# A four-layer mixer network on one core: the conditioning products, each quarter of TensorE given its own columns

## The chip, the cores and the metric

The kernel runs on one NeuronCore of a Trainium2 chip. The metric is the device time of one execution in microseconds (us). The kernel is written out by hand for five instruction queues: TensorE (PE, with its weight loads shown as PEld), VectorE (DVE), ScalarE (ACT), GpSimd (POOL) and SyncE (SP), which issues most of the DMAs. The queues meet at semaphores only; each runs its own list in order.

## The reference

A sequence of 256 latent tokens and 256 context tokens of width 1024 goes through four conditioned layers and then two more sublayers on the latent tokens (a mixer of three branches and a feed-forward net). The four conditioned layers differ in their mixer (window attention, latent attention, mLSTM, window attention) but share one frame:

```
def rmsnorm(x, g):
    xf = x.astype(jnp.float32)
    y = xf * lax.rsqrt(jnp.mean(xf * xf, axis=-1, keepdims=True) + EPS)
    return (y * g.astype(jnp.float32)).astype(x.dtype)
```

Each layer has a matrix `w_ada` of 1024 x 3072 and a bias `b_ada`. Two vectors (one for the latent tokens from `c`, one for the context tokens from `c_ctx`) go through silu and are multiplied with `w_ada`. The 3072 results are, for each of the two, a shift, a scale and a gate of 1024 each. Before the mixer the normalised rows become `norm(x) * (1 + scale) + shift`; after it, its normalised output is multiplied by the gate and added to `x`. The whole is in float32.

The change concerns only how the product with `w_ada` is laid out and turned.

## The kernel before

**Weights.** All weights pass through a ring of six slots (`NR`), in blocks of 512 KB, [128, 1024] float32. SyncE's `w_load` loads block j when block j - 6 has been used. For ordinary blocks ScalarE rounds a high part (`w_h`, `w_round`) and VectorE makes the rest (`w_l`, `w_rest`); conditioning blocks are used raw. `Weights.next` hands out a block and lets the splits run up to `ahead` blocks ahead, so a split that comes early waits in ScalarE's queue for its load. The first 15 blocks of layer 0's conditioning lie in places of their own (`aside`).

**The product.** Only two of the rows of the stationary operand carry anything: `cT` is [128, 8, 32], with two used columns, one for each condition. A matmul of 32 stationary columns fills a quarter of TensorE's columns and writes 32 partitions. `ada_mm` (L2235) puts four such products into the four quarters, each with other rows (another k of 128) of the same 256 columns. A block holds four k and 256 columns. Four blocks (two halves of columns, two sets of rows) fill a group's bank of 512 columns, with four partial sums on partitions 0, 32, 64, 96 (and 1, 33, 65, 97 for the context). float32 products go through TensorE in two passes, so a block shows as eight weight loads.

**After it.** Groups 0 to 3 of a layer are shift and scale: ScalarE copies the bank to `stage` (`ada_row`), and `ada_turn` (L2242) makes four products with `stage` as the stationary operand and the two-column selector `sel` as the moving one, which adds the four partial sums and puts the columns on partitions. VectorE adds the bias and the gain in `ada_add` (L2909). Groups 4 and 5 are the gate: ScalarE copies them to `gt_rows`, a DMA puts the bias on row 2, `gate_split` makes a high part `l_gth` (ScalarE) and a rest `gt_rest` (VectorE), both [128, 1024], and `gate_spread` (L2249) multiplies a broadcast selector with both to put the sum on all partitions, 512 columns at a time, four times a layer; VectorE multiplies each by the gain into `l_G`.

**Order.** The generator `ada` (L533) yields after each block and is woven by `weave` into the units of an attention: `weave(att, ada, num, den)` lets `num` steps of `ada` run per `den` units and drains what is left at the end. It runs in the second attention call of layer 0 (gate of 0, shift and scale of 1), in layer 1's attention (gate of 1, rest of 2), among the mLSTM chunks of layer 2 (`paced` by two; gate of 2, rest of 3) and in the second attention call of layer 3 (gate only, 10 steps to 16 units). Turns come `lag` steps after their group, gate steps 0 to 4 come 10, 12, 14, 16 and 18 steps after the gate's second group. All take one of the two banks PAIR = (0, 1), one of which a group in progress holds. Layer 0's own shift and scale are computed at the start (`layer_first`), group by group, between the first rows and the first products of layer 0.

## Time and profile before

| | us |
|---|---|
| median of three runs | 1579.5 (1578.32 to 1583.96) |
| the profiled execution | 1581.7 |
| its span, first to last instruction | 1579.9 |
| TensorE busy | 1483.3 (94%) |
| VectorE busy | 1000.6 (63%) |
| ScalarE busy | 766.0 (48%) |
| mean granted TensorE clock | 0.984 of full |

Busy time counts an instruction from its start to its end; on TensorE the ends are modelled and neighbours overlap, so what an operation costs there is read from one start of a weight load to the next. "Granted clock" is the share of the full TensorE clock of 2.4 GHz. A row's bracket says how long the engine stood before it and who released it; "issue" is no wait on another engine. A row's line number can be that of a helper (L2207 all products, L2210 all transposes, L2515 ScalarE copies, L2872 VectorE operations on two tensors), so operations are told apart by tile names.

### The profile page before, as it was taken

How to read it: one execution, taken by the hardware profiler on the slowest of the kernel's cores; microseconds unless marked ns; L12 is line 12 of the kernel's file. 1: busy time of each engine (PE TensorE's matmuls, PEld its weight loads, DVE VectorE, ACT ScalarE, POOL GpSimd, SP SyncE). 2: the span in 40 equal slices, each digit the busy share in tenths (PEclk: the TensorE clock that was granted, in tenths of full speed). 3: DMA queues.
4: the chain of work that ended last, by engine and by line, in shares of the span. 5: the costliest groups of instructions: out<-in, count | busy, mean ns of one | idle time of the engine just before them, and what ended most of it. 6: DMA issues, size and time to landing. Idle time of an engine off the chain costs nothing.

```text
span 1579.9 us, 24093 instructions
## 1 busy us (share of the span) xinstructions
PE 1483.3 (94%) x9344; PEld 1205.7 (76%) x9344; DVE 1000.6 (63%) x2304; ACT 766.0 (48%) x1640; POOL 67.5 (4%) x76
## 2 busy tenths in 40 slices
PE   6999998999999999999998999888899999989999
PEld 4787756787778777888766777666687789789987
DVE  3647677464667458635576667666786557777753
ACT  4436576353556344332224545565666437455542
POOL 0000000010000000020000100001100120000000
PEclk9999999999999999999989999999999999999999
DMA  9131172222452232221371134423435552445554
GB/s 358 55 107 54 50 244 95 76 92 80 138 184 94 70 111 93 91 83 54 123 264 53 54 130 126 144 84 123 152 133 160 182 182 94 147 156 191 188 187 134
DMA packets 59842, 202.84 MB, mean 128 GB/s; under 512 B 7682, under 2 KB 10956, under 8 KB 59600
## 3 DMA queue, kind: packets, MB, share of 16 engines
q1 hardware_dynamic: 53568, 192.84, 35.6%
q10 hardware_dynamic: 5984, 7.40, 2.0%
q8 instruction: 75, 1.23, 0.3%
q0 software_dynamic: 176, 1.06, 0.2%
q14 instruction: 39, 0.32, 0.1%
HBM read 199.42 MB, written 1.84 MB: 127 GB/s over the span
## 4 chain that ended last, share of the span: by engine, by line
PE 72%; DVE 15%; ACT 5%; DMA 3%; issue 3%; POOL 1%; ACTq 0%; SPq 0%; POOLq 0%; DVEq 0%
PE ps L2207 66%; PE ps L2210 5%; DVE w_l L2872 3%; DMA w_raw<-in_l_out 1%; DVE st L2968 1%; ACT w_h L2515 1%; DVE x L2880 1%; DVE l_h_lat L2880 1%; DMA w_l_ada<-in_l_ada 1%; DVE m_P L3452 1%; ACT l_P L2518 1%; DVE l_xn L2876 1%; DMA w_raw<-in_l_z 1%; DVE l_P L2876 1%; POOL mstat L3546 0%
## 5 line engine op out<-in xcount | busy, mean ns | idle before, releaser
L2872 DVE TENSOR_TENSOR w_l<-w_raw,w_h 128x1024 fp32r<-128x1024 f32 (+3 forms) x263 | 314.8, 1206 | 76.6 <-ACT w_h L2515 76.1
L2515 ACT ACTIVATE w_h<-w_raw 128x1024 fp32r<-128x1024 f32 (+3 forms) x263 | 271.3, 1042 | 112.9 <-DMA w_raw<-in_l_out 26.3
L2207 PE MATMUL ps<-w_h,l_hTh 128*128 128x512 f32 (+1 forms) x384 | 157.2, 410 | 0.3 <-DVE w_l L2872 0.2
L2207 PE MATMUL ps<-w_h,l_hTl 128*128 128x512 f32 (+1 forms) x384 | 152.8, 398 | 0.0
L2207 PE MATMUL ps<-w_l,l_hTh 128*128 128x512 f32 (+1 forms) x384 | 152.7, 398 | 0.0
L2518 ACT ACTIVATE l_P<-ps,st 128x512 f32<-128x512 f32 (+1 forms) x128 | 77.5, 607 | 82.3 <-DVE st L2880 55.0
L2207 PE MATMUL ps<-f_hTh,w_h 128*128 128x256 f32 x352 | 99.0, 281 | 0.0
L2207 PE MATMUL ps<-f_hTl,w_h 128*128 128x256 f32 x352 | 98.9, 281 | 0.0
L2207 PE MATMUL ps<-f_hTh,w_l 128*128 128x256 f32 x352 | 98.9, 281 | 0.0
L2968 DVE TENSOR_REDUCE st<-ps 128x1 f32<-128x512 f32 (+2 forms) x112 | 72.8, 650 | 40.4 <-PE ps L2207 39.7
L2207 PE MATMUL ps<-l_hTh,w_h 128*128 128x512 f32 (+1 forms) x264 | 97.5, 369 | 0.5 <-issue 0.5
L2207 PE MATMUL ps<-l_hTl,w_h 128*128 128x512 f32 (+1 forms) x264 | 96.9, 367 | 0.0
L2207 PE MATMUL ps<-l_hTh,w_l 128*128 128x512 f32 (+1 forms) x264 | 96.9, 367 | 0.0
L2207 PEld LDWEIGHTS ps<-w_h,l_hTl 128*128 128x128 f32 x384 | 73.3, 191 | 16.7
L2207 PEld LDWEIGHTS ps<-w_h,l_hTh 128*128 128x128 f32 x384 | 73.5, 191 | 15.2 <-issue 1.2
L2207 PEld LDWEIGHTS ps<-w_l,l_hTh 128*128 128x128 f32 x384 | 73.4, 191 | 14.5
L2207 PE MATMUL ps<-l_PT,l_V 128*64 128x128 f32 (+1 forms) x712 | 69.9, 282 | 3.1 <-DVE l_ogf L2880 3.1
L2207 PEld LDWEIGHTS ps<-l_PT,l_V 128*64 128x64 f32 (+1 forms) x712 | 55.6, 151 | 21.4 <-issue 13.4
L2210 PE MATMUL ps<-cst,l_P 128*128 128x128 f32 x416 | 67.1, 281 | 4.5 <-ACT l_PT L2515 1.7
L2207 PEld LDWEIGHTS ps<-f_hTh,w_h 128*128 128x128 f32 x352 | 67.1, 190 | 0.2 <-issue 0.2
L2207 PEld LDWEIGHTS ps<-f_hTl,w_h 128*128 128x128 f32 x352 | 67.0, 190 | 0.0
L2207 PEld LDWEIGHTS ps<-f_hTh,w_l 128*128 128x128 f32 x352 | 66.9, 190 | 0.0
(444 smaller groups left out, 3484.4 us busy)
## 6 DMA issues: line engine op xcount, KB each, us to landing
w_raw<-in_l_ada SPq DMA_DIRECT2D x81, 512.0 KB, 4.3
w_raw<-in_l_z SPq DMA_DIRECT2D x32, 512.0 KB, 3.6
w_raw<-in_l_out SPq DMA_DIRECT2D x32, 512.0 KB, 3.7
w_raw<-in_m_merge SPq DMA_DIRECT2D x24, 512.0 KB, 3.3
w_raw<-in_f_gate SPq DMA_DIRECT2D x22, 512.0 KB, 3.3
w_raw<-in_f_up SPq DMA_DIRECT2D x22, 512.0 KB, 3.3
w_raw<-in_f_down SPq DMA_DIRECT2D x22, 512.0 KB, 4.3
w_raw<-in_l_q SPq DMA_DIRECT2D x16, 512.0 KB, 3.7
```

What stands on the lines that cost most here:

```text
L2207: return p.e.matmul(out, lhsT, rhs, start=start, stop=stop)
L2210: return p.e.transpose(out, a, ident)
L2515: return p.e.activation(out, a, func, scale=scale)
L2518: return p.e.activation(out, a, func, bias=bias, scale=scale, accum_out=accum)
L2872: return p.e.tensor_tensor(out, a, b, op)
L2876: return p.e.tensor_scalar(out, a, s1, None, op0)
L2880: return p.e.scalar_tensor_tensor(out, a, s, b, op0, op1)
L2968: p.e.reduce_max(soft.stat(u, 0, nh), ps if nh == 1 else ps.rearrange("p (h k) -> p h k", h=nh), AX.X).then_inc(*p.mark(*soft.key("peak", u)))
L3452: v = p.e.tensor_tensor_reduce(dst, src, bias[i], 1.0, -3.0e38, ALU.add, ALU.max, mx[:, i:i + 1])
```

## The change

A block of shift and scale holds k outermost: one k of 1024 columns (512 of shift, 512 of scale) in layers 1 to 3, two k of 512 columns (256 and 256) in layer 0. The four quarters of TensorE work on the same k and on different columns: 256 each in layers 1 to 3, 128 each in layer 0. The eight k are summed in the bank, so that a group of eight blocks (four in layer 0) uses 256 (128) columns of it, and a layer has two groups (layer 0 four). Partition 32 j + v has the results of quarter j for condition v. The turn is a transpose of each 128 columns (two in a group, one in layer 0), from which VectorE takes the columns that matter through a strided view. The gate is one group of eight blocks, [128, 256]; its bias goes to partitions 2, 34, 66, 98; its high part and rest are 256 wide, and a spread makes four products of 256 columns with a selector for quarter and condition. The generator yields after every second block, `lag` is 2 of these steps, gate steps come one after another, and the weaves have 14 steps in each of the three attentions; layer 2's is no longer paced. In layer 0's opening the order is kept. Left out below: the size of `selr`, the file's other changed call of `aside`.

```diff
+ADA = (256, 512, 512, 512)
...
-    ada = [_r(o + 256 * b, o + 256 * b + 256) for b in range(4) for o in (0, 1024)] + _split(_r(2048, 3072), 256)
+    both = lambda a, b: np.concatenate([_r(a, b), _r(1024 + a, 1024 + b)])
-        add(f"l{i}_ada", f"l{i}_w_ada", ada, 4, D)
+        add(f"l{i}_ada", f"l{i}_w_ada", [both(a, a + ADA[i]) for a in range(0, 1024, ADA[i])], 1024 // (2 * ADA[i]), D)
+        add(f"l{i}_adg", f"l{i}_w_ada", [_r(2048, 3072)], 1, D)
...
-    sel = np.zeros((128, 2), np.float32)
-    sel[[0, 32, 64, 96], 0] = 1
-    sel[[1, 33, 65, 97], 1] = 1
+    sel = np.zeros((128, 8), np.float32)
+    for j in range(4):
+        for lc in range(2):
+            sel[[32 * j + lc, 32 * j + 2], 2 * j + lc] = 1
-    c["selb"] = sel + np.where(np.arange(128) == 2, 1, 0)[:, None].astype(np.float32)
...
-        self.gt, self.gtl = self.at("gt_rows", [128, D], F32, at), self.at("gt_rest", [128, D], F32R, at)
+        self.gt, self.gtl = self.at("gt_rows", [128, 256], F32, at), self.at("gt_rest", [128, 256], F32R, at)
...
-    def ada(p, pool, groups, gate=None, steps=(), lag=2, ahead=AHEAD, blocks=(), late=None):
+    def ada(p, pool, groups, gate=None, lag=2, ahead=AHEAD, blocks=(), late=None):
...
-        for i, b in groups:
+        for i, g in groups:
-            for half in range(2):
-                for r in range(2):
-                    x = (2 * b + half) * 2 + r
-                    c = blocks.pop(0) if blocks else p.W.next(f"l{i}_ada", x, 4, 256, raw=True, ahead=ahead)
-                    key = ("ada", "mm", i, x)
-                    p.ada_mm(key, c, bank, half, r)
-                    c.free = key
+            w = 256 if g == "gate" else ADA[i] // 2
+            name, ks = f"l{i}_ada" if g != "gate" else f"l{i}_adg", 256 // w
+            nb = 8 // ks
+            for r in range(nb):
+                x = r if g == "gate" else g * nb + r
+                c = blocks.pop(0) if blocks else p.W.next(name, x, ks, 4 * w, raw=True, ahead=ahead)
+                key = ("ada", "mm", i, g, r)
+                p.ada_mm(key, c, bank, r, ks, w)
+                c.free = key
+                if r < nb - 1 and (late is not None or r % 2):
-                    if late is None or half + r < 2:
-                        yield
-            if b < 4:
+                    yield
+            if g != "gate":
-                v = ("ada", "row", i, b)
-                p.ada_row(v, bank, s, key, p.stage_tok[s])
-                then = lambda i=i, b=b, s=s, v=v: p.ada_mod(i, b, s, v, pool)
+                v = ("ada", "row", i, g)
+                p.ada_row(v, bank, s, w, key, p.stage_tok[s])
+                then = lambda i=i, g=g, s=s, v=v, w=w: p.ada_mod(i, g, s, w, v, pool)
-                v = ("ada", "gate_row", i, b)
-                p.ada_gate_row(v, bank, b, key)
+                v = ("ada", "gate_row", i)
+                p.ada_gate_row(v, bank, key)
-            if b == 5:
+            if g == "gate":
-                wait += [[10 + 2 * x, lambda x=x: gate.step(x, pool)] for x in steps]
-            if late is not None:
-                yield
+                wait += [[5 + x, lambda x=x: gate.step(x, pool)] for x in range(5)]
+            tick()
+            yield
-    def ada_mod(p, i, b, s, v, pool):
+    def ada_mod(p, i, g, s, w, v, pool):
-        p.stage_tok[s] = ("ada", "col", i, b)
-        p.ada_turn(p.stage_tok[s], mb, s, v)
-        t, u, w = ("ada", "shift", i, b), ("ada", "scale0", i, b), ("ada", "scale", i, b)
-        p.ada_add(t, u, w, i, b, mb, p.stage_tok[s])
+        p.stage_tok[s] = ("ada", "col", i, g)
+        p.ada_turn(p.stage_tok[s], mb, s, w, v)
+        t, u, x = ("ada", "shift", i, g), ("ada", "scale0", i, g), ("ada", "scale", i, g)
+        p.ada_add(t, u, x, i, g, w, mb, p.stage_tok[s])
-        p.mod_ready[i, b] = [t, w]
+        n = w // 128
+        for kp in range(n * g, n * g + n):
+            p.mod_ready[i, kp] = [t, x]
     def staged(p, n_units, lead, ring, soft, peak, cols, late, lag=1, early=True):
...
-        gpost, gth = at("gpost", [128, D], F32, gpost), at("gth", [128, D], F32R, gth)
+        gpost, gth = at("gpost", [128, D], F32, gpost), at("gth", [128, 256], F32R, gth)
...
-        groups = [(i, 4), (i, 5)] + ([(i + 1, b) for b in range(4)] if i < 3 else [])
+        groups = [(i, "gate")] + ([(i + 1, 0), (i + 1, 1)] if i < 3 else [])
-        weave(att, p.ada(PAIR, groups, Gate(p, i, *gate, f), range(5), lag=3), 4 * len(groups) + 2, steps)
+        weave(att, p.ada(PAIR, groups, Gate(p, i, *gate, f)), 14, steps)
...
-        weave(m.attention(f), p.ada(PAIR, [(1, 4), (1, 5)] + [(2, b) for b in range(4)], gate, range(5), lag=3), 28, 32)
+        weave(m.attention(f), p.ada(PAIR, [(1, "gate"), (2, 0), (2, 1)], gate), 14, 32)
...
-        mod = paced(p.ada(PAIR, [(3, 0), (3, 1), (2, 4), (2, 5), (3, 2), (3, 3)], gate, range(5), lag=3, ahead=2), 2)
+        mod = p.ada(PAIR, [(3, 0), (2, "gate"), (3, 1)], gate, ahead=2)
...
-    def ada_mm(p, key, c, bank, half, r):
+    def ada_mm(p, key, c, bank, r, ks, w):
-        p.wait_ge(c.ready, ("begin", "cT"), p.B.freed[bank] if half + r == 0 else None)
-        for j in range(4):
-            m = p.mm(n.ps[32 * j:32 * j + 32, bank, half * 256:half * 256 + 256], n.cT[:, 4 * r + j, :], c.raw[:, j], r == 0, r == 1)
+        p.wait_ge(c.ready, ("begin", "cT"), p.B.freed[bank] if r == 0 else None)
+        for s in range(ks):
+            k = ks * r + s
+            for j in range(4):
+                m = p.mm(n.ps[32 * j:32 * j + 32, bank, 0:w], n.cT[:, k, :], c.raw[:, s, w * j:w * j + w], k == 0, k == 7)
-    def ada_turn(p, key, mb, s, v):
+    def ada_turn(p, key, mb, s, w, v):
-        for j in range(4):
-            m = p.mm(out[:, 2 * j:2 * j + 2], n.stage[s][:, j * 128:j * 128 + 128], n.c["sel"], True, True)
+        for j in range(w // 128):
+            m = p.tr(out[:, 128 * j:128 * j + 128], n.stage[s][:, j * 128:j * 128 + 128], n.c["ident"])
     def gate_spread(p, gate, bank, lc, b, tok, g):
-        n, i, c = p.n, gate.i, slice(b * 512, b * 512 + 512)
-        sel = n.selr[:, lc:lc + 1].to_broadcast([128, 128])
+        n, i = p.n, gate.i
-        p.mm(n.bank(bank), sel, gate.gth[:, c], True, False)
-        p.wait_ge(("gate", "l", i))
-        p.mm(n.bank(bank), sel, n.gtl[:, c], False, True).then_inc(*p.mark(*tok))
+        for y in range(2):
+            j, out = 2 * b + y, n.bank(bank)[:, 256 * y:256 * y + 256]
+            sel = n.selr[:, 2 * j + lc:2 * j + lc + 1].to_broadcast([128, 128])
+            p.mm(out, sel, gate.gth[:], True, False)
+            p.wait_ge(("gate", "l", i))
+            m = p.mm(out, sel, n.gtl[:], False, True)
+        m.then_inc(*p.mark(*tok))
     def rows_turn(p, rows, ts, kp, b):
...
-    def ada_row(p, key, bank, s, tok, stage_tok):
+    def ada_row(p, key, bank, s, w, tok, stage_tok):
-        p.copy(p.n.stage[s][:], p.n.bank(bank)).then_inc(*p.mark(*key))
-    def ada_gate_row(p, key, bank, b, tok):
+        p.copy(p.n.stage[s][:, 0:w], p.n.bank(bank, w)).then_inc(*p.mark(*key))
+    def ada_gate_row(p, key, bank, tok):
-        p.copy(p.n.gt[:, b * 512 - 2048:b * 512 - 1536], p.n.bank(bank)).then_inc(*p.mark(*key))
+        p.copy(p.n.gt[:], p.n.bank(bank, 256)).then_inc(*p.mark(*key))
-        row = p.n.dram[f"l{i}_b_ada"].unsqueeze(0)[:, 2048:3072]
+        rows = p.n.dram[f"l{i}_b_ada"][2048:3072].rearrange("(j c) -> j c", j=4)
-        p.e.dma_start(p.n.gt[2:3, :], row).then_inc(*p.landed("d_gate_bias", i))
+        p.e.dma_start(p.n.gt[2:99:32, :], rows).then_inc(*p.landed("d_gate_bias", i))
...
-        p.copy(n.selr[:], n.c["selb"]).then_inc(*p.mark("begin", "const"))
+        p.copy(n.selr[:], n.c["sel"]).then_inc(*p.mark("begin", "const"))
...
-    def ada_add(p, t, u, w, i, b, mb, tok):
-        n, mod, out, k = p.n, p.n.mod[i % 2], p.n.bank(mb), slice(2 * b, 2 * b + 2)
-        bc = lambda name: n.v[name][:, k].unsqueeze(2).to_broadcast([128, 2, 2])
-        pv = out[:, 0:8].rearrange("p (a k v) -> p a k v", a=2, v=2)
+    def ada_add(p, t, u, x, i, g, w, mb, tok):
+        n, c = p.n, w // 128
+        k = slice(2 * c * g, 2 * c * g + 2 * c)
+        mod, out = n.mod[i % 2][:, :, k], n.bank(mb)[:, 0:w].rearrange("p (c a q y) -> p a c q y", c=c, a=2, q=2)
+        to = mod.rearrange("p a (q c) v -> p a c q v", q=2)
+        bc = lambda name: n.v[name][:, k].unsqueeze(2).to_broadcast([128, 2 * c, 2])
+        of = lambda name: bc(name).rearrange("p (q c) v -> p c q v", q=2)
-        p.tt(mod[:, 0, k], pv[:, 0], bc(f"l{i}_b_sh"), ALU.add).then_inc(*p.mark(*t))
-        p.tt(mod[:, 1, k], pv[:, 1], bc(f"l{i}_b_sc"), ALU.add).then_inc(*p.mark(*u))
+        p.tt(to[:, 0], out[:, 0, :, :, 0:2], of(f"l{i}_b_sh"), ALU.add).then_inc(*p.mark(*t))
+        p.tt(to[:, 1], out[:, 1, :, :, 0:2], of(f"l{i}_b_sc"), ALU.add).then_inc(*p.mark(*u))
-        p.stt(mod[:, 1, k], mod[:, 1, k], 1.0, bc(f"l{i}_g_pre"), ALU.add, ALU.mult).then_inc(*p.mark(*w))
+        p.stt(mod[:, 1], mod[:, 1], 1.0, bc(f"l{i}_g_pre"), ALU.add, ALU.mult).then_inc(*p.mark(*x))
     def gate_split(p, gate, gt_tok):
```

## Rows read from the trace of the kernel before

**Rows 1.** The page, chain of work that ended last, shares by engine.
```profile
PE 72%; DVE 15%; ACT 5%; DMA 3%; issue 3%; POOL 1%; ACTq 0%; SPq 0%; POOLq 0%; DVEq 0%
```

**Rows 2.** Stages: length, busy of PE, PEld, DVE, ACT, POOL, clock, DMA share, GB/s.
```profile
20.00:52.00 32.00, 29.85 (x217) 21.59 (x216) 16.84 (x36) 15.20 (x25) 0.00 (x0) 1.00 0.69 269
202.00:236.00 34.00, 33.46 (x335) 20.11 (x334) 26.83 (x96) 25.67 (x82) 0.00 (x0) 1.00 0.78 268
...
423.00:500.00 77.00, 76.92 (x630) 58.91 (x629) 53.17 (x190) 45.18 (x125) 0.00 (x0) 1.00 0.53 177
...
817.00:833.00 16.00, 13.22 (x94) 9.49 (x86) 11.50 (x25) 9.22 (x15) 0.00 (x0) 0.79 0.58 205
...
1047.00:1054.00 7.00, 4.24 (x23) 2.79 (x20) 4.24 (x10) 4.41 (x6) 0.00 (x0) 0.87 0.01 2
```

**Rows 3.** Timeline of TensorE's weight loads, layer 0's second attention call.
```profile
207.61 0.42 PEld L2210 LDWEIGHTS ps<-cst,l_P 128*128 128x128 f32 x4 [0.41 <-DVE l_P L2876]
...
208.78 0.16 PEld L2207 LDWEIGHTS ps<-w_raw,cT 128*32 128x32 f32 x8 [0.24 <-issue]
209.35 0.42 PEld L2210 LDWEIGHTS ps<-cst,l_P 128*128 128x128 f32 x4 [0.41 <-DVE l_P L2876]
209.74 0.19 PEld L2207 LDWEIGHTS ps<-l_kTh,l_qT 128*128 128x128 f32 x1
...
217.84 0.19 PEld L2207 LDWEIGHTS ps<-l_kTh,l_qT 128*128 128x128 f32 x1
217.96 0.19 PEld L2207 LDWEIGHTS ps<-l_kTl,l_qT 128*128 128x128 f32 x1
218.29 0.16 PEld L2207 LDWEIGHTS ps<-w_raw,cT 128*32 128x32 f32 x8
...
222.61 0.59 PEld L2207 LDWEIGHTS ps<-w_raw,cT 128*32 128x32 f32 x16
223.61 0.85 PEld L2207 LDWEIGHTS ps<-l_PT,l_V 128*64 128x64 f32 x16 [0.41 <-DVE l_ogf L2880]
```

**Rows 4.** The same timeline, layer 1's attention.
```profile
462.77 0.97 PEld L2207 LDWEIGHTS ps<-cst,stage 128*128 128x128 f32 x8 [0.41 <-issue]
463.65 0.97 PEld L2207 LDWEIGHTS ps<-l_PT,l_V 128*128 128x128 f32 x8
...
477.56 0.18 PEld L2207 LDWEIGHTS ps<-l_gth,selr 128*128 128x128 f32 x1 [0.41 <-issue]
...
477.90 0.64 PEld L2207 LDWEIGHTS ps<-l_PT,l_V 128*128 128x128 f32 x4
```

**Rows 5.** A ScalarE copy of 128x128 out of a bank: duration in ns, min/median/max.
```profile
L2515 ACT ACTIVATE m_bv<-ps x2: 268/272/277, 1107.6 to 1108.3; 128x128 f32<-128x128 f32 x2
```

**Rows 6.** The chain in order of time, layer 0's opening.
```profile
34.55 0.60 ACT stage L2515
...
35.20 1.05 PE ps L2207 x8
```

**Rows 7.** The chain in order of time, end of layer 3's second attention call.
```profile
1048.44 0.95 ACT l_gth L2515
...
1049.42 1.24 DVE gt_rest L2872
...
1051.24 0.70 DVE l_G L2872
```

**Rows 8.** Weight loads, end of layer 0's second attention call.
```profile
256.98 0.18 PEld L2207 LDWEIGHTS ps<-l_gth,selr 128*128 128x128 f32 x1 [1.56 <-DVE l_G L2872]
...
260.67 0.97 PEld L2207 LDWEIGHTS ps<-cst,stage 128*128 128x128 f32 x8 [1.59 <-ACT stage L2515]
```

**Rows 9.** Weight loads, first product of layer 3's output projection.
```profile
1053.33 0.33 PEld L2207 LDWEIGHTS ps<-w_h,l_qT 128*128 128x128 f32 x1
```

**Rows 10.** Timeline of VectorE, layer 0's second attention call.
```profile
208.17 0.16 DVE L2880 SCALAR_TENSOR_TENSOR st<-st,l_sink 128x1 f32<-128x1 f32 x1
...
209.75 0.16 DVE L2880 SCALAR_TENSOR_TENSOR st<-st,l_sink 128x1 f32<-128x1 f32 x1
```

More of the change, by code:

```diff
@@ L278, in place @@
         self.identb = self.at("identb", [128, 128], BF16, self.here(256))
-        self.selr = self.new("selr", [128, 2], F32R)
+        self.selr = self.new("selr", [128, 8], F32R)
         self.phalf = self.new("phalf", [128, 8])
@@ L668, in layer_first @@
         places = [base + 1024 * k for k in (52, 56, 60, 64, 68, 72, 76, 80, 84, 88, 92, 96, 115, 119, 123)]
-        blocks, late = [p.W.aside("l0_ada", x, 4, 256, at) for x, at in enumerate(places)], []
+        blocks, late = [p.W.aside("l0_ada", x, 2, 512, at) for x, at in enumerate(places)], []
         p.begin_loads(blocks)
```

## The prediction

> **What bounds the kernel now.** I read the chain of work that ended last first: 72% of the span is TensorE [rows 1], so what counts is time taken from TensorE where it is the last to arrive, and from ScalarE or VectorE only where they are. Then the table of stages [rows 2] for the five places in which the conditioning (the "ada" work) is done: the opening of layer 0 (20 to 52 us), the second attention call of layer 0 (202 to 262), the attention of layer 1 (423 to 500), the mLSTM chunks of layer 2 (to 833) and the second attention call of layer 3 (to 1054). In 423 to 500 TensorE is busy 76.92 of 77 us, in 202 to 236 33.46 of 34: there every TensorE nanosecond counts. After 236 the gate steps load VectorE too and I take the bound as mixed. In 1047 to 1054 TensorE works 4.24 of 7 us: something is waited for. Last, the weight-load timeline of TensorE, since start to start of loads is what an operation costs there (the durations of matmuls include their latency).
>
> **Part 1: two blocks per step.** The matmuls for layers 1 to 3 and for the gates stay the same in number and shape (four quarters, 32 stationary and 256 moving columns); only the meaning of a quarter changes. A lone block takes 0.57 us, 208.78 to the next load at 209.35; two in a row take 1.00 us, 222.61 to 223.61 [rows 3]. So the block proper is 0.43 and leaving the quarter layout costs 0.14. Entering costs too: two loads of the scores lie 0.12 apart (217.84, 217.96), but the ada block after them starts 0.33 later: 0.21. A pair therefore saves 0.14 + 0.21 = 0.35 us, where full-width work stands on both sides. Where the next work is the value product of layer 0 with its 64-column tiles, a change of layout is paid anyway, and I take 0.14. Before, a step has one block: layer 0 has 24 blocks in 23 runs (the pair at 222.61 is its one double step), layer 1 24 in 24, layer 3 8 in 8; after: 12, 12 and 4 runs. Layer 2 had its steps paced by two already and gains nothing here. Layer 1: 12 x 0.35 = 4.2. Layer 0: 11 fewer, about half of each kind, 11 x 0.25 = 2.8. Layer 3: 4 x 0.25 = 1.0. The weights come as before in 512 KB blocks, six slots ahead. The DMA share of 0.78 in 202 to 236 [rows 2] leaves room for a step of two blocks every 1.7 attention units, so I cost the transfers at nothing; without that cover each late pair would stand in TensorE's queue and hold the scores behind it.
>
> **Part 2: the turn.** Before, four groups per layer, each four fp32 products with two columns, eight loads: 462.77 to 463.65 = 0.88 us [rows 4]. After, layers 1 to 3 have two groups, each two transposes of 128x128. Four such transposes take 209.35 to 209.74 = 0.39 [rows 3], so two take 0.2. Per layer 4 x 0.88 - 2 x 0.2 = 3.1 us of TensorE in layers 0 (for layer 1's weights) and 1. In layer 2 the last turn runs where the granted clock was 0.79 of full [rows 2], so I take 3.6. ScalarE's copies ahead of it go from four of 128x512 to two of 128x256: between 0.27 (a 128x128 copy, [rows 5]) and 0.60 [rows 6]; I take 0.38.
>
> **Part 3: the gate.** Gate rows are 256 wide on 128 partitions instead of 1024 wide: one copy of about 0.38 instead of two of 0.60, the high part 0.95 becomes about 0.4 and the rest 1.24 becomes about 0.4 [rows 7] (estimates, by size between the same rows). The spread becomes four products of 256 columns instead of two of 512: before 477.56 to 477.90 = 0.34 us [rows 4], after 4 x 0.12 (spacing of 256-column products, [rows 3]) = 0.48. That is +0.14, four times a layer: +0.55. The products into G on VectorE (0.70, [rows 7]) stay. The bias comes in one DMA as before, four rows of 1 KB, four steps ahead of its use: nothing. In layer 1 the load of the post gains is still issued with gate step 0 and has one step of 2.3 units where it had two of 1.1: nothing either.
>
> **Part 4: order.** Gate steps now come one step apart instead of two and start after step 8 of about 14. Two consequences. In layers 0 and 1, spread 1 and the turn of the first group fall into the same step, while the running group holds the other of the two PAIR banks, so the turn waits until VectorE has multiplied the spread; behind it in TensorE's queue stand the next unit's transposes and scores, and VectorE's next maximum waits for those. Waits of that kind were up to 1.56 us [rows 8]; I take +1.0 in each of layers 0 and 1. In layer 3 the pace was 10 steps for 16 units, so gate split and spreads came after the attention, with nothing beside them: high part from 1048.44, rest from 1049.42 [rows 7], first product of the output projection at 1053.33, with a load of 0.33 instead of 0.19 [rows 9, 3], that is at the half clock. After, the gate steps fall on yields 9 to 14 of about 22 and are woven in. TensorE may start the output at about 1048.8: 4.5 us, and about 1.0 for the half clock at the start. Against that, VectorE gets 4 x 0.70 + 0.4 = 3.2 us inside an attention that is already bound by the three engines in turns. At the end of layer 0's call the last turn waited 1.59 us for its copy [rows 8]; it now falls inside the weave: -1.6.
>
> **Part 5: opening of layer 0.** Four groups as before; each block has eight products of 128 columns instead of four of 256. On the chain each group has a copy of 0.60 and a turn of 1.05 [rows 6]. After: copy 0.27, one transpose 0.1 plus the same latency, about 0.27. So 1.1 per group. The first group's gain I give to the wait for the next weights, with DMA at 0.69 of its time in this stretch [rows 2]; three count: 3.3. The finer products cost: a 128-column pass with its load is like a transpose, 0.10 to 0.11, so 4 x 0.11 = 0.44 per block against 0.43, +0.2 for twelve blocks. The other bound is that loads don't hide: 0.16 for the eight of a block [rows 3] on each of four passes, +0.65 per block, +7.8 in all. Since transposes with whole 128x128 loads run at 0.10, I take the low end. Net -3.0.
>
> The Trainium skill, TensorEngine Tiling (Array Packing), section Instruction Overhead, says every matmul carries some 60 cycles and that tiling should not shorten a dimension that is already small. It speaks against the 128-column products: as an estimate by that page, eight more hardware products in a block at 25 ns each are 0.2 us, 2.4 us for twelve blocks, and the forecast would be 1562. The spacing of the transposes in this trace [rows 3] shows 0.10 for a load and 128 columns together, so I see no such sum on top.
>
> **The sum.** Opening -3.0. Layer 0 attention, TensorE: -2.8 - 3.1 + 0.55 + 1.0 - 1.6 = -6.0; but in its first units VectorE is close behind: its units follow 1.58 us apart without a gap (208.17 to 209.75 [rows 10]) against 1.74 on TensorE (207.61 to 209.35), so only 0.16 of a unit can be won there; I take -4.5. Layer 1: -4.2 - 3.1 + 0.55 + 1.0 = -5.8, less 0.6 for uneven steps, as two score banks bind units without a block: -5.2. Layer 2: -3.6 + 0.55 and about 1.4 less on ScalarE and VectorE in the tail, where both are waited for; part is hidden behind weights landing: -3.1. Layer 3: -5.5 + 3.2 - 1.0 - 0.2 for copies: -3.5. Total -19.3 us. The profiled execution took 1581.7 for a span of 1579.9 and would become 1562.4; the median of the runs is 1579.5, 2.2 below it. Forecast: **1560**.
>
> **The rivals.**
> VectorE takes over as the bound (chance 0.22): in layers 0 and 3 the saved TensorE time turns into waits for VectorE. For it: 1.58 of 1.74. Against it: VectorE works 26.83 of 34 us. It leaves 1.5 in each of these layers: 3.0 + 1.5 + 5.2 + 3.1 + 1.5 = 14.3, so 1565.
> Small gain (0.12): the loads of the 128-column passes show, so the opening costs 7.8 - 3.3 = 4.5; layer 0's attention gives 2, layer 1 3, layer 2 1 and layer 3 3, each cut by uneven steps. Together -4.5: 1575.
> The bank wait (0.05) is the slower side: spreads and turns share one bank of PAIR while a group holds the other for four steps. Each use may wait for VectorE's product, 1.56 as in [rows 8]. Uses per layer: five, in layers 0, 1 and 2: fifteen. At 1.3 us each the gain is gone, at 1.8 the kernel is slower by 0.5%; with 2 us each it is 1590. Against it: one step is now 1.7 units or more, some 3 us, longer than VectorE's lag.
> The clock (0.03): the turns no longer keep TensorE as active and it falls to the half level around the opening. The stage shows 1.00 granted (2.4 GHz) with the same pauses [rows 2]. If its 29.85 us of TensorE work ran at 1.2 GHz, 29.9 us would be added and the other stages' 16.3 remain: 1593. The Trainium skill, TensorE: Matmul & The Clock Gate, section Part 4: PE-mode transpose, states that transposes don't count as activity for the clock; no row here isolates that, and the transposes of the attention run at 1.00.
>
> **How the numbers follow.** Forecast as told 0.58, own range 1552 to 1566. With nothing held back it is -3.0 - 1.1 - 6.0 - 1.1 (every pair of layer 0 at 0.35) - 5.8 - 4.5 - 6.5 (layer 3 with its added VectorE work hidden) = -28: 1551.5. Those bounds, the VectorE case and the near edge of the small gain give the range 1551 to 1573. 0.5% of this kernel, 7.9 us, is about what a measurement tells from no change. Faster: 0.58 + 0.22 = 0.80; same 0.12; slower 0.05 + 0.03 = 0.08.
>
> **What would show it.** Right: ada runs of 16 loads in the attentions, each about 1.0 to the next load; two turns a layer of 0.2; layer 1's stage 5 us shorter; no gate work between the last attention unit and the output projection of layer 3; the groups of the opening 1.0 us closer together. Wrong: passes of 128 columns above 0.15 apart, turns that wait over 1.5 us for the spread's product, scores that wait for VectorE after each lone unit, or weights that land late after a double step.

## The result, and the profile after

In six runs of each the changed kernel took 1573.3 us (1570.8 to 1575.5) and the kernel before 1580.4 (1577.4 to 1584.6): ratio 0.9956, 95% interval 0.9940 to 0.9972. A second series with ten runs of the changed kernel gave 0.9945 (0.9926 to 0.9963). So the change brings some 7 us where 19 were forecast. The profiled execution took 1573.1 us for a span of 1571.3; its mean granted clock was 0.980 of full.

The page's chain of waits for the changed kernel has the shares of [rows 1] nearly unmoved:

```profile
PE 71%; DVE 15%; ACT 5%; DMA 4%; issue 3%; POOL 1%; ACTq 0%; SPq 0%; DVEq 0%; POOLq 0%
```

To see where time went I took places that both traces have: the first product after the last turn of the opening, and for the three attention calls the first load of scores and the first load of the output projection behind them. The times in brackets are those places in the kernel before.

| stretch | before | after | difference | forecast |
|---|---|---|---|---|
| opening, to the last group's first product | 47.09 | 44.01 | -3.1 | -3.0 |
| layer 0, second call (201.58 to 267.96) | 66.4 | 63.3 | -3.1 | -4.5 |
| layer 1, attention (420.91 to 506.65) | 85.7 | 82.1 | -3.6 | -5.2 |
| layer 3, second call (1009.98 to 1053.33) | 43.3 | 48.0 | **+4.6** | -3.5, with the head of the projection |

Layer 2 gained 3.2 (forecast 3.1), and in layer 3 the head of the projection, now at full clock, gained 1.1 more. Added up, the stages give -9.5 us where -19.3 was forecast; of the 9.8 that are missing, 7.0 are layer 3's, 1.6 layer 1's and 1.4 layer 0's. The spans of the two profiled executions differ by 8.6 us; that of before was taken somewhat above its median. The stages of work answer to [rows 2] so (busy time of each engine, granted clock, DMA):

```profile
core 0: us, PE busy (x) PEld busy (x) DVE busy (x) ACT busy (x) POOL busy (x), PEclk, DMA share, GB/s
202.00:236.00 34.00, 32.67 (x338) 21.16 (x342) 27.52 (x99) 25.27 (x82) 0.00 (x0) 1.00 0.80 289
250.00:262.00 12.00, 8.48 (x89) 6.25 (x90) 8.92 (x38) 8.53 (x30) 0.00 (x0) 1.00 0.01 1
418.00:497.00 79.00, 76.25 (x651) 62.32 (x652) 54.86 (x199) 44.43 (x131) 0.00 (x0) 1.00 0.48 167
985.00:1003.00 18.00, 14.86 (x140) 10.46 (x139) 10.70 (x38) 8.59 (x25) 0.00 (x0) 0.96 0.44 126
1003.00:1022.00 19.00, 14.12 (x85) 8.24 (x85) 10.13 (x28) 10.44 (x26) 0.00 (x0) 0.68 0.71 240
1022.00:1044.00 22.00, 20.13 (x196) 15.62 (x196) 18.13 (x62) 15.30 (x44) 0.00 (x0) 1.00 0.00 1
```

The row from 1003 to 1022 is the odd one: VectorE and ScalarE work little more than half of it, TensorE 14.1 of 19 us, the granted clock is 0.68, and DMA is busy 0.71 of the time. Lined up by VectorE's maxima, the changed kernel leads by 12.3 us at its 1006.8 and by 5.3 at the next one, its 1015.6. ScalarE's timeline shows what happened in between:

```profile
1005.81 0.28 ACT L2531 ACTIVATE st<-st,l_sink 128x1 f32<-128x1 f32 x1
1010.26 1.06 ACT L2529 ACTIVATE w_h<-w_raw 128x1024 fp32r<-128x1024 f32 x1 [4.17 <-DMA w_raw<-in_l_out]
1011.22 0.58 ACT L2529 ACTIVATE l_PT<-ps 128x512 f32<-128x512 f32 x1
...
1012.54 2.00 ACT L2529 ACTIVATE w_h<-w_raw 128x1024 fp32r<-128x1024 f32 x2
1014.44 0.38 ACT L2529 ACTIVATE gt_rows<-ps 128x256 f32<-128x256 f32 x1
```

ScalarE stands 4.17 us at the rounding of a block of the output projection whose load has not landed. Behind it in its queue stand the copy of the transposed probabilities (`l_PT`), the next exponentials (`l_P`) and the gate rows. VectorE and TensorE follow; first VectorE, then TensorE's weight loads:

```profile
1011.35 1.23 DVE L2886 TENSOR_TENSOR w_l<-w_raw,w_h 128x1024 fp32r<-128x1024 f32 x1 [3.66 <-ACT w_h L2529]
```

```profile
1007.42 0.16 PEld L2216 LDWEIGHTS ps<-w_raw,cT 128*32 128x32 f32 x8 [0.57 <-DMA w_raw<-in_l_adg]
...
1011.91 0.72 PEld L2219 LDWEIGHTS ps<-cst,l_P 128*128 128x128 f32 x4 [2.98 <-issue]
...
1016.15 0.72 PEld L2219 LDWEIGHTS ps<-cst,l_P 128*128 128x128 f32 x4 [2.54 <-DVE l_P L2890]
...
1044.00 0.19 PEld L2216 LDWEIGHTS ps<-w_h,l_qT 128*128 128x128 f32 x1 [0.17 <-issue]
```

Four transposes' loads take 0.72 where they take 0.42 at full clock, so TensorE is at the lower level (1.2 GHz) behind the pauses. The last row stands where [rows 9] had a load of 0.33: the projection now starts right behind the attention and at full clock.

Why was the load late? SyncE's queue in this stretch:

```profile
998.09 0.80 SPq L3635 DMA_DIRECT2D w_raw<-in_l_adg  x2
1001.97 6.48 SPq L3635 DMA_DIRECT2D w_raw<-in_l_out  x6
```

and the last line of the view of the tile `w_raw` (996 to 1016), which covers two gate blocks and six output blocks:

```profile
DMA to landing us min/median/max: 6.5/8.5/9.0
```

The eight gate blocks are used between 997.4 and 1008.1. Each frees a slot; six loads of 512 KB go out within 6.5 us and take 7.8 to 9.0 each, while over the whole program the blocks of this weight take 4.5 in the median. `Weights.next` lets the splits run three blocks ahead of the block in use, so using the last gate blocks puts output blocks, freshly requested, into ScalarE's list. The kernel before had its first such rounding at 1029.8, without a wait.

The six loads were not alone. From the views of the DMA issues of 985 to 1060, the changed kernel:

```profile
w_raw<-in_l_out SPq DMA_DIRECT2D x8, 512.0 KB, 8.2
...
m_BTb<-m_biasb ACTq DMA_DIRECT2D x4, 256.0 KB, 6.6
...
l_gpost<-in_l_g_post ACTq DMA_DIRECT2D x1, 512.0 KB, 12.6
```

and the kernel before:

```profile
w_raw<-in_l_out SPq DMA_DIRECT2D x7, 512.0 KB, 4.3
```

Both kernels issue four bias loads and the post gains from ScalarE's queue 1.2 to 3.0 us into this call. Before, the first output block was requested 9.7 us into the call and its rounding stood in ScalarE's list at 19.8; in the changed kernel these are 6.0 and 10.1. So the faster pace also moved the output loads up behind these 1.5 MB: from 1001 to 1008 the DMA engines are busy all the time (share 1.04) and move 275 GB/s. No run moves these five loads, so how much of the 8.5 us is theirs and how much the six loads' own is open.

**Layers 0 and 1.** The collision of spread and turn is there, once a layer (weight loads of TensorE, layer 0 and layer 1):

```profile
228.76 0.59 PEld L2216 LDWEIGHTS ps<-w_raw,cT 128*32 128x32 f32 x16 [0.24 <-issue]
229.76 0.18 PEld L2216 LDWEIGHTS ps<-l_gth,selr 128*128 128x128 f32 x1 [0.41 <-issue]
...
230.10 0.19 PEld L2216 LDWEIGHTS ps<-gt_rest,selr 128*128 128x128 f32 x1
231.82 0.20 PEld L2219 LDWEIGHTS ps<-cst,stage 128*128 128x128 f32 x2 [1.53 <-DVE l_G L2886]
232.19 0.42 PEld L2216 LDWEIGHTS ps<-l_PT,l_V 128*64 128x64 f32 x8 [0.17 <-issue]
```

```profile
417.90 0.19 PEld L2216 LDWEIGHTS ps<-l_knh,l_qnh 128*128 128x128 f32 x1 [1.07 <-ACT l_P L2532]
...
463.69 0.20 PEld L2219 LDWEIGHTS ps<-cst,stage 128*128 128x128 f32 x2 [1.04 <-DVE l_G L2886]
463.86 0.97 PEld L2216 LDWEIGHTS ps<-l_PT,l_V 128*128 128x128 f32 x8
...
484.81 0.86 PEld L2216 LDWEIGHTS ps<-l_PT,l_V 128*128 128x128 f32 x7 [1.13 <-ACT l_PT L2529]
```

A step of two blocks is 1.00 and a turn about 0.2 to 0.4, as forecast. What is new is at the end of layer 0's call, where no block is left to fill TensorE's pauses. The last turn's wait for its copy did shrink, from 1.59 to 0.22:

```profile
248.70 0.20 PEld L2219 LDWEIGHTS ps<-cst,stage 128*128 128x128 f32 x2 [0.22 <-ACT stage L2529]
250.19 0.42 PEld L2219 LDWEIGHTS ps<-cst,l_P 128*128 128x128 f32 x4 [1.30 <-DVE l_P L2890]
252.04 0.19 PEld L2216 LDWEIGHTS ps<-l_kTh,l_qT 128*128 128x128 f32 x1 [1.43 <-ACT l_P L2532]
...
254.87 0.42 PEld L2219 LDWEIGHTS ps<-cst,l_P 128*128 128x128 f32 x4 [0.72 <-DVE st L2985]
...
257.01 0.42 PEld L2219 LDWEIGHTS ps<-cst,l_P 128*128 128x128 f32 x4 [0.70 <-DVE st L3005]
```

**Opening** (weight loads, third group; [rows 6] has the chain of before):

```profile
31.65 1.69 PEld L2216 LDWEIGHTS ps<-w_l_ada,cT 128*32 128x32 f32 x64 [0.37 <-issue]
34.00 0.14 PEld L2219 LDWEIGHTS ps<-cst,stage 128*128 128x128 f32 x1 [0.67 <-ACT stage L2529]
34.06 0.91 PEld L2219 LDWEIGHTS ps<-cst,l_xn 128*128 128x128 f32 x8
```

The same group in the kernel before:

```profile
32.55 1.45 PEld L2207 LDWEIGHTS ps<-w_l_ada,cT 128*32 128x32 f32 x32 [0.37 <-issue]
35.20 0.97 PEld L2207 LDWEIGHTS ps<-cst,stage 128*128 128x128 f32 x8 [1.20 <-ACT stage L2515]
```

The turn is one load, 0.06 before the next work, in place of eight, and the wait for its copy is 0.67 in place of 1.20.

### The profile page after: what moved, and what is told of

Its sections match the earlier page's. It is cut to its first block, busy times and chain, and to the rows that moved or that the text cites. A ratio compares the mean times of both kernels' runs of the same rounds, so it can differ in the third digit from the quotient of the medians.

```text
span 1571.3 us, 24144 instructions
## 1 busy us (share of the span) xinstructions
PE 1469.6 (94%) x9392; PEld 1204.5 (77%) x9392; DVE 995.1 (63%) x2286; ACT 755.6 (48%) x1630; POOL 67.5 (4%) x76
## 4 chain that ended last, share of the span: by engine, by line
PE 71%; DVE 15%; ACT 5%; DMA 4%; issue 3%; POOL 1%; ACTq 0%; SPq 0%; DVEq 0%; POOLq 0%
PE ps L2216 65%; PE ps L2219 5%; DVE w_l L2886 2%; DVE st L2985 1%; DMA w_raw<-in_l_out 1%; DVE x L2894 1%; ACT w_h L2529 1%; DVE l_P L2890 1%; ACT l_P L2532 1%; DMA w_l_ada<-in_l_ada 1%; DVE m_P L3469 1%; DVE l_xn L2890 1%; DVE l_h_lat L2894 1%; POOL mstat L3563 1%; POOL pstat L3574 1%
## 5 line engine op out<-in xcount | busy, mean ns | idle before, releaser
L2219 PEld LDWEIGHTS ps<-cst,l_P 128*128 128x128 f32 x416 | 47.2, 143 | 26.0 <-DVE l_P L2890 10.6
```

The costliest lines, as they stand in the source:

```text
L2219: return p.e.transpose(out, a, ident)
```

## The experiments

Theory after the first look: layer 3 loses to ScalarE's queue, because the faster pace brings the splits ahead of their loads. Rival: VectorE, which now has the gate work inside the attention. All lengths below are between the places of the table; the ratios are to the kernel before.

### Where layer 3's time went

Splits held back (`e1`):

```diff
-        weave(att, p.ada(PAIR, groups, Gate(p, i, *gate, f)), 14, steps)
+        weave(att, p.ada(PAIR, groups, Gate(p, i, *gate, f), ahead=0 if i == 3 else AHEAD), 14, steps)
```

> The changed kernel, but in layer 3 no split of an output-projection weight block is queued on ScalarE or VectorE while the gate blocks are consumed; all of them come at the head of the output projection. Theory (ScalarE stands in its queue 4.17 us at a split whose load has not landed, and the attention stands behind it): the units of layer 3 from 1011 us on keep the lead of 14 us that they had before the stall, so the attention ends about 6 us earlier; the first product of the projection then waits for one rounding (1.05) and one rest (1.22), 2.3 us. Net 3 to 5 us faster than the changed kernel, near 1569. Rival (VectorE's gate work inside the attention is the cost): the stall moves but the time stays within 1 us of the changed kernel, or is 2.3 us worse.

Ratio 0.9919 (0.9888 to 0.9950), which overlaps the changed kernel's interval; the trace tells more. The call with the wait at its end is 42.7 long instead of 48.0. ScalarE has no wait for a load in the attention, and the projection behind it takes 1.5 longer than in the changed kernel, at the lower clock for a part. The price of the late rounding appears where it was foreseen, somewhat higher (weight loads):

```profile
1039.33 0.19 PEld L2216 LDWEIGHTS ps<-w_h,l_qT 128*128 128x128 f32 x1 [3.20 <-ACT w_h L2529]
```

One gate block per step in layer 3 (`e2`), the gate steps one apart, and 15 steps instead of 14 in that call:

```diff
-                if r < nb - 1 and (late is not None or r % 2):
+                if r < nb - 1 and (late is not None or (i == 3 and g == "gate") or r % 2):
...
-                wait += [[5 + x, lambda x=x: gate.step(x, pool)] for x in range(5)]
+                wait += [[(3 if i == 3 else 5) + x, lambda x=x: gate.step(x, pool)] for x in range(5)]
...
-        weave(att, p.ada(PAIR, groups, Gate(p, i, *gate, f)), 14, steps)
+        weave(att, p.ada(PAIR, groups, Gate(p, i, *gate, f)), 14 if i < 3 else 15, steps)
```

> The changed kernel, but the eight gate blocks of layer 3 come one per step (so over about 9 units instead of 4.6), the gate steps behind them one apart as before. The splits stay where the changed kernel has them relative to the blocks. Theory (the pace brought the splits ahead of their loads): the load of each output block has twice the time, the wait of 4.17 us on ScalarE goes, and four more changes of layout cost about 1.0: 4 to 6 us faster than the changed kernel, near 1568. Rival (VectorE's gate work): no gain, and 1 us lost to the added steps.

Ratio 0.9899 (0.9874 to 0.9924); the call is 42.8. With twice the time the same roundings find their loads landed (ScalarE):

```profile
1011.99 1.04 ACT L2529 ACTIVATE w_h<-w_raw 128x1024 fp32r<-128x1024 f32 x1
...
1014.27 1.05 ACT L2529 ACTIVATE w_h<-w_raw 128x1024 fp32r<-128x1024 f32 x1
...
1016.77 1.04 ACT L2529 ACTIVATE w_h<-w_raw 128x1024 fp32r<-128x1024 f32 x1
```

Splits held back, with the edit of `e1`, and three of them put between the last gate steps (`e6`):

```diff
+        n = 0
         while wait:
             tick()
+            n += 1
+            if ahead == 0 and 2 <= n <= 4:
+                p.W.split_to(p.W.rounded, p.W.rounded - 1)
             yield
```

> As the run with the splits of layer 3 held back, but three of them are queued one per step behind gate steps, when their loads have landed, as the kernel before had three of them inside its attention. Theory (queue): no wait for a load on ScalarE and no exposed rounding at the projection's head: 6 to 7 us faster than the changed kernel, near 1566.5. Rival (VectorE's gate work): within 1 us of it.

Ratio 0.9897 (0.9873 to 0.9920); the call is 42.0, which is 6.0 less than in the changed kernel, though VectorE still has all the gate work in it. The rival would have left it where it was. The window with the wait:

```profile
1003.00:1022.00 19.00, 17.18 (x145) 10.94 (x144) 14.98 (x43) 14.12 (x35) 0.00 (x0) 0.97 0.67 232
```

DMA is nearly as busy (0.67 for 0.71), TensorE works 17.2 of 19 us instead of 14.1, and the clock is 0.97 instead of 0.68. So the long fall of the clock came with the wait and goes with it.

The pace alone, put into the kernel before (`e10b`):

```diff
-        weave(att, p.ada(PAIR, groups, Gate(p, i, *gate, f), range(5), lag=3), 4 * len(groups) + 2, steps)
+        weave(att, p.ada(PAIR, groups, Gate(p, i, *gate, f), range(5), lag=3), 4 * len(groups) + 2 if i < 3 else 28, steps)
```

> The kernel before with one thing of the change: in layer 3 the gate blocks come at 28 steps for 16 units instead of 10, which is the changed kernel's pace in blocks, so that gate steps too fall into the attention. Layout, turns and one block per step stay. Theory (the pace brings the splits ahead of their loads): ScalarE waits for a w_raw of the output weights inside the attention and the stretch from 985 to 1070 us gets 2 to 5 us longer, as in the changed kernel. Rival (the new gate rows or the double step did it): it stays or gets shorter, since the gate tail after the attention goes away.

Ratio 1.0028 (1.0005 to 1.0050): slower than the kernel before, though barely clear of it, with the old layout and the old turns. The call is 51.6 instead of 43.3, more than the 2 to 5 expected. ScalarE waits twice:

```profile
1011.45 0.28 ACT L2517 ACTIVATE st<-st,l_sink 128x1 f32<-128x1 f32 x1
1016.51 1.06 ACT L2515 ACTIVATE w_h<-w_raw 128x1024 fp32r<-128x1024 f32 x1 [4.78 <-DMA w_raw<-in_l_out]
1018.57 1.06 ACT L2515 ACTIVATE w_h<-w_raw 128x1024 fp32r<-128x1024 f32 x1 [1.01 <-DMA w_raw<-in_l_out]
```

TensorE, too, stands 2.95 us for the load of a conditioning block here, and VectorE has gate work inside the attention as in the changed kernel, so this run alone sets a size for none of them. It shows that the layout isn't needed for the loss; `e1`, `e2` and `e6`, which keep VectorE's work, show that this work isn't the cause. Together: it is the pace against the loads of the ring.

### Layers 0 and 1

The collision taken away (`e3`), by moving the gate steps of layers 0 and 1 one step on:

```diff
-                wait += [[5 + x, lambda x=x: gate.step(x, pool)] for x in range(5)]
+                wait += [[5 + x + (i < 2), lambda x=x: gate.step(x, pool)] for x in range(5)]
```

> The changed kernel with the gate steps of layers 0 and 1 one step later, so that no spread falls into the step of the first group's turn. Theory (bank collision): the waits of TensorE at the turn for VectorE's product (1.53 us at 231.8 and 1.04 at 463.7) go, so layer 0's attention ends 1.5 us and layer 1's 1.0 us earlier, 2.5 in all or less where VectorE binds anyway. Rival (layer 0 is bound by VectorE, so the wait is no loss): the wait turns up elsewhere and under 0.5 us is gained.

Layer 0 is 62.1 (1.2 less), layer 1 80.8 (1.3 less); the ratio 0.9915 (0.9886 to 0.9944) can't tell it from the changed kernel by itself, the trace can. The turn comes right behind its block (weight loads, layer 0):

```profile
229.77 0.59 PEld L2216 LDWEIGHTS ps<-w_raw,cT 128*32 128x32 f32 x16 [0.24 <-issue]
230.77 0.20 PEld L2219 LDWEIGHTS ps<-cst,stage 128*128 128x128 f32 x2 [0.41 <-issue]
```

One block per step again (`e4`):

```diff
-                if r < nb - 1 and (late is not None or r % 2):
+                if r < nb - 1:
...
-                wait += [[5 + x, lambda x=x: gate.step(x, pool)] for x in range(5)]
+                wait += [[10 + 2 * x, lambda x=x: gate.step(x, pool)] for x in range(5)]
...
-        weave(att, p.ada(PAIR, groups, Gate(p, i, *gate, f)), 14, steps)
+        weave(att, p.ada(PAIR, groups, Gate(p, i, *gate, f)), 28, steps)
```

(and the same in layer 1, with the lag of the turns 4 instead of 2; layer 2 `paced` by two).

> The changed kernel with one block per step again everywhere (28 steps where it has 14, the turns and gate steps at the same distance in blocks), layer 2 still by two. Own theory of the forecast: a lone step costs 0.35 us of TensorE in layer 1 and 0.25 in layer 0, so layer 1's attention gets 4 us longer, layer 0's 3 us, layer 3's 1 us: 8 us slower than the changed kernel in these stages. From the rows of both kernels (12 entries of about 0.30 over a plain score load, and twice 0.57 against 1.00 behind) the price in layer 1 would be 5. Rival (VectorE binds layer 0): layer 1 gets 4 us longer, layer 0 under 1.5 us.

Layer 1 is 1.8 longer (83.9), layer 0 0.5 (63.9), layer 3 0.4: under both forecasts of the price. Ratio 0.9962 (0.9941 to 0.9984).

The turn by products (`e5`), the new layout kept:

```diff
-            m = p.tr(out[:, 128 * j:128 * j + 128], n.stage[s][:, j * 128:j * 128 + 128], n.c["ident"])
+            m = p.mm(out[:, 8 * j:8 * j + 8], n.stage[s][:, j * 128:j * 128 + 128], n.c["sel"], True, True)
```

(and the view that VectorE reads, eight columns a piece).

> The changed kernel with its turns made by fp32 products with eight selecting columns instead of transposes (the layout stays). A product with its two loads was 0.22, a transpose 0.10: two more tenths per turn of two, +0.5 a layer in layers 0 to 2, +0.1 and a little latency for each of the four groups of the opening: 1.5 to 2.5 us slower in all. That is the part of the turn's gain that is the transpose's; the rest would belong to the layout, which needs 4 pieces a layer where the kernel before turned 16. Rival (transposes are what pays): 6 us or more slower.

Layer 1 is 82.3, 0.2 longer; ratio 0.9943 (0.9920 to 0.9965), the same as the changed kernel's, where 1.5 to 2.5 us more were expected. Layer 0's call is 64.9, but its last units had a granted clock of 0.72, as in `e6` (its row is below), so it says nothing of the turn. The transpose as such is worth next to nothing in layer 1: the turn got cheap because the layout leaves 4 pieces of 128 columns a layer to be turned where there were 16.

Less work for TensorE (`e7`): columns of the conditioning products left out.

```diff
+                u = 64 if w == 256 and key[2] in (1, 2) and key[3] != "gate" and 0 < k < 7 else w
-                m = p.mm(n.ps[32 * j:32 * j + 32, bank, 0:w], n.cT[:, k, :], c.raw[:, s, w * j:w * j + w], k == 0, k == 7)
+                m = p.mm(n.ps[32 * j:32 * j + 32, bank, 0:u], n.cT[:, k, :], c.raw[:, s, w * j:w * j + u], k == 0, k == 7)
```

> The changed kernel, but of the conditioning products for layers 1 and 2 six of eight blocks of each group multiply only 64 of each quarter's 256 columns (the rest is left out). That takes about 0.32 us of TensorE from each of 12 blocks, 3.9 us from each of the attentions of layers 0 and 1, and nothing from the other engines or the queues. TensorE as the bound: both stages get 3 to 3.9 us shorter. VectorE as layer 0's bound: layer 0 under 1.5 us shorter, layer 1 3 or more.

Of some 3.9 us taken from TensorE in each, layer 1 gets 3.2 shorter and layer 0 0.4. In layer 0 the wait at the turn grows from 1.53 to 2.49:

```profile
231.63 0.20 PEld L2219 LDWEIGHTS ps<-cst,stage 128*128 128x128 f32 x2 [2.49 <-DVE l_G L2887]
```

Less work for VectorE (`e9b`): three quarters of each maximum left out.

```diff
-        p.e.reduce_max(soft.stat(u, 0, nh), ps if nh == 1 else ps.rearrange("p (h k) -> p h k", h=nh), AX.X).then_inc(
-            *p.mark(*soft.key("peak", u)))
+        ps = ps.rearrange("p (h k) -> p h k", h=nh)
+        if soft.tag[0] in (0, 1):
+            ps = ps[:, :, 0:w // 4]
+        p.e.reduce_max(soft.stat(u, 0, nh), ps, AX.X).then_inc(*p.mark(*soft.key("peak", u)))
```

> The changed kernel, but in layers 0 and 1 the softmax maximum of a unit is taken over the first quarter of each head's scores (the other three quarters are left out of the maximum). That takes about 0.4 us off each of VectorE's reductions of 0.69 us and shortens the way from scores to the exponentials by as much; TensorE's work is untouched. If layer 0's attention is held by VectorE and the way through it, its stage (out-projection to out-projection) gets 3 us or more shorter; if TensorE holds layer 1, that stage gets under 1.5 us shorter. If TensorE holds both, both stay within 1 us.

Layer 0 is 1.7 shorter (61.6), layer 1 0.9. Neither reading of layer 0 holds by itself: VectorE loses some 9 us of work there (24 reductions, 0.69 to 0.29) and 1.7 come back. In the windows of the last units (250 to 262) `e7`, `e9b` and `e6` have a clock that the changed kernel's profile doesn't have; `e6`'s row, with the same work in layer 0 as the changed kernel:

```profile
250.00:262.00 12.00, 9.72 (x70) 7.59 (x68) 9.20 (x37) 8.34 (x29) 0.00 (x0) 0.72 0.04 16
```

Its call is 64.9 instead of 63.3, so such a fall costs 1.6. A shorter one costs nothing that can be seen: the kernel with both repairs (`e8`, below) has the same instructions in layer 0 as `e3`, whose clock is 1.00 here, and both calls are 62.1 long. `e8`'s row:

```profile
250.00:262.00 12.00, 9.77 (x87) 7.56 (x88) 8.55 (x37) 8.64 (x30) 0.00 (x0) 0.86 0.00 0
```

`e9b` (0.88 in this window) has such a shorter fall, so its 1.7 can stand as read. `e7` has one too (0.86) and another behind the turn's wait (0.95 from 202 to 236), so its 0.4 may be too small by an amount that no run shows.

An even pace (`e12`), on top of both repairs: 13 steps instead of 14 in layers 0 and 1.

> The kernel with both repairs, and in layers 0 and 1 the conditioning woven at 13 instead of 14 steps over the call, so that its last steps reach the last unit. Theory (in the last third of layer 0's call the three engines wait for one another because nothing fills TensorE's pauses): the blocks end about one unit later, one or two of the pauses of 0.7 to 1.4 us after 250 us are filled, layer 0's stage is 0.5 to 1.5 us shorter than with both repairs, layer 1's within 0.5. Rival (VectorE or the spreads' order sets the end): within 0.5 us or worse, because the last gate step then stands behind the last unit.

No gain: layer 0 62.2 (62.1 with both repairs), layer 1 81.5 (80.8), ratio 0.9894 (0.9865 to 0.9923). A pause of 2.7 us before a spread took the place of the pauses it filled.

### Repeat, and both repairs

> The changed kernel once more, unaltered, on a chip with other runs. Its stage differences to the kernel before should repeat within 0.3 us where the clock is the same (layer 0 -3.1, layer 1 -3.6, layer 3 +3.5 us). A clock that falls at the end of layer 0's attention, as in two other runs, would give layer 0 -1.5.

Layer 0 63.3, layer 1 82.1, layer 3's call 48.0, opening at 43.8: the stages repeat within 0.2. Over all runs with the change the opening's end lies between 43.1 and 44.5, so its gain is 2.6 to 4.0.

Both repairs (`e8`) are the edits of `e3` and of `e6` together.

> The changed kernel with both repairs: in layer 3 three splits held back to the steps behind the gate blocks, and the gate steps of layers 0 and 1 one step later. If the two losses are separate, layer 3 is 6 to 7 us shorter, layer 0 1.2 and layer 1 1.3: near 1564, about 9 faster than the changed kernel. If they are one loss seen twice, not faster than the run with the splits alone (1566.8).

1563.1 us beside 1583.7 for the kernel before: ratio 0.9868 (0.9842 to 0.9894), clear of the changed kernel's interval in either series. Layer 0 62.1, layer 1 80.8, layer 3 41.9: both losses are separate and both come back. This version beats both kernels.

## Why the prediction was wrong

**The step that failed** is in part 1: "The DMA share of 0.78 in 202 to 236 [rows 2] leaves room for a step of two blocks every 1.7 attention units, so I cost the transfers at nothing". It was said of all layers and read from layer 0. In layer 3 the eight gate blocks come in four steps of two at the start of the call, the loads behind them are the output projection's, and those are not used raw: ScalarE rounds them three blocks ahead, in its strict queue. Part 4 counted what the moved gate steps cost VectorE and left out that the faster pace moves the splits too. Instead of -3.5 layer 3 gave +3.5 (4.6 in the call, less 1.1 behind it). With the splits put right (`e6`) it gives 1.3 in the call and 1.1 behind, -2.5 in all, so 2.5 of the 3.5 that part 4 saw were real, and one unpriced wait of 4.17 us, with what it held up behind it, ate them.

**Opening**: -3.1 for -3.0. The 128-column products cost little: 64 loads span 1.69 us where 32 of before span 1.45 for the same four blocks, 0.24 more, or 0.7 for the twelve blocks where 0.2 was forecast. By the estimate from the Trainium skill, TensorEngine Tiling (Array Packing), section Instruction Overhead, four blocks would have cost 0.8 more and the gain would have been 2.4 us less; this trace doesn't show that.

**Layer 1**, -3.6 for -5.2. Summing start to start over the loads of the call, turns gave -3.05 (forecast -3.1), the collision +1.1 (+1.0), the spreads +0.4 (+0.55). What is left for the two-block steps is -2.1 for -4.2, and `e4` says 1.8. The price of leaving the quarter layout was read rightly (the loads of the blocks take 1.8 less, 12 x 0.14 was 1.7), but 2.1 us came back, most of it in two waits for ScalarE in units that now have no block, the 1.07 at 417.90 and the 1.13 at 484.81; I had put 0.6 there. The step that was mis-sized is the term for uneven steps.

**Layer 0**, -3.1 for -4.5. The wait at the collision was 1.5 and not 1.0 (1.2 came back in `e3`), and `e4` puts the two-block steps at 0.5 where I took 2.8: the mis-sized term. `e7` shows why: of 3.9 us of TensorE's time only 0.4 came back there, even if part was lost to the clock. VectorE alone doesn't hold it either (`e9b`); from 250 us on the engines wait for each other in turn. The rival "VectorE takes over" left layer 0 a gain of 1.5 and the forecast 4.5; the measured 3.1 lies halfway, and the rival is only partly right about the engine.

**Layer 2**: -3.2 for -3.1. 2.9 of it is there at 802 us of the kernel before, with a clock of 1.00 in both profiles up to 810. Behind that the clock falls at different places, and such falls alone move the stage by as much as 1.4: `e10b`, whose instructions there are those of the kernel before, is 1.4 faster than it between 775 and 870. So the gain is real and the agreement to 0.1 is luck.

**The rivals.** "Small gain" said 1575 and came within 2 us of the measured time, but not by its mechanism: it had the opening 4.5 us slower, and it was 3.1 faster, and it had layer 3 3 us faster, where 3.5 were lost. **The bank wait** as slower rival: one collision a layer in layers 0 and 1, not fifteen. **The clock**: the opening stayed at 1.00; it fell in layer 3, behind the stall.

Where exactly layer 0's last units lose time is open: the runs show that neither TensorE's nor VectorE's work alone decides it, and `e12`, that an even pace doesn't mend it.

## What to carry to other kernels

When work that uses blocks of a ring is made faster, ask what those blocks' successors are and who touches them next: a transfer is hidden only as long as no in-order queue has an instruction on it that arrives before it lands. Check that in each stage by itself; room in one stage (DMA 0.78 of layer 0) says nothing of another, and other loads that go out in the same stretch count too. And before a cheaper operation is given the credit, run it in the old form within the new layout: here the layout had turned 16 pieces into 4, and the transpose added 0.2 us in layer 1.

## What was unexpected of the hardware

Six loads of 512 KB issued within 6.5 us, behind 1.5 MB of other loads, took 7.8 to 9.0 us each, where the median of this weight's loads over the program is 4.5. And the same instructions in layer 0's last units ran at a granted clock of 1.00 in four profiles (the changed kernel, its repeat, `e1`, `e2`) and at 0.72 from 250 to 262 in another (`e6`), for 1.6 us; `e3` and `e8` differ in the same way (1.00 and 0.86), for nothing. The stretch is full of pauses of 0.7 to 1.4 us; what tips it one way or the other the profiles don't show.
